# A two-layer decoder trunk: the next stage's first weight slot ahead of the third norm, x turned in four banks, conditioning steps respread, matrix heads scaled on ScalarE

## What is computed

```
mod = silu(c) @ ada_w[layer] + ada_b[layer]        # six rows of 1024: shift, scale, gate twice
h   = x * (1 + scale) + shift
y   = mixer(h)   or   (silu(h @ w1) * (h @ w3)) @ w2
x   = LayerNorm(alpha * x + (1 + gate) * y) * g + b
```

```
num, den = weighted sums over the past            # den from a column of ones
hid = num / max(|den|, exp(-m))
out = sigmoid(o) * head_norm(hid) * ml_g           # mean and variance over the 128 of a head
y   = concat(gla_out, out) @ w_out
```

## Time and profile before

| | |
|---|---|
| median of 3 runs (lowest, highest) | 1455.12 us (1454.17, 1455.47) |
| the profiled execution | 1455.61 us |
| its span | 1453.8 us |
| mean granted TensorE clock | 0.968 |
| TensorE matmul busy | 1369.1 us (94%) |
| VectorE busy | 635.6 us (44%) |
| GpSimd busy | 512.0 us (35%) |
| ScalarE busy | 453.2 us (31%) |

### The profile page before, as it was taken

One profiled execution on the slowest core, in us unless ns is written; L12 is line 12 of the kernel. 1 busy time (PEld: TensorE's weight loads), 2 busy tenths in 40 slices (PEclk: granted clock), 3 DMA queues, 4 the chain that ended last, 5 costly groups with the idle time before them and its releaser, 6 DMA issues.

```text
span 1453.8 us, 17178 instructions
## 1 busy us (share of the span) xinstructions
PE 1369.1 (94%) x6566; PEld 1130.1 (78%) x6566; DVE 635.6 (44%) x835; ACT 453.2 (31%) x606; POOL 512.0 (35%) x209
## 2 busy tenths in 40 slices
PE   7899999979999999999899999998889999999995
PEld 6778777759888888888788777788678888887884
DVE  3579635779443343400882243357484011010007
ACT  2343243424222223122422344315243232232121
POOL 2343312223434435444244222120225444444440
PEclk9999999999999999999999999998999999999998
DMA  9592524241654646743225311111113232334312
GB/s 332 147 121 83 202 101 79 97 166 52 231 194 152 231 167 208 176 128 102 106 102 192 120 48 40 58 44 44 58 58 104 100 101 90 98 97 139 96 58 58
DMA packets 93521, 173.81 MB, mean 120 GB/s; under 512 B 15719, under 2 KB 61943, under 8 KB 93340
## 3 DMA queue, kind: packets, MB, share of 16 engines
q1 hardware_dynamic: 90328, 169.63, 37.7%
q10 hardware_dynamic: 3140, 3.43, 0.8%
HBM read 170.87 MB, written 4.52 MB: 121 GB/s over the span
## 4 chain that ended last, share of the span: by engine, by line
PE 67%; issue 21%; POOL 6%; DVE 5%; ACT 1%; POOLq 0%; DVEq 0%; ACTq 0%
PE ps L1043 13%; PE ps L1044 13%; PE ps L1045 13%; PE ps L1075 6%; PE ps L1076 6%; PE ps L1077 6%; POOL w_lo L677 6%; PE ps L1199 1%; PE ps L1532 1%; PE ps L1200 1%; PE ps L1201 1%; PE ps L1558 1%; PE ps L1546 1%; PE ps L1543 1%; DVE rec L2224 1%
## 5 line engine op out<-in xcount | busy, mean ns | idle before, releaser
L677 POOL TENSOR_TENSOR w_lo<-raw,w_hi 128x1024 fp32r<-128x1024 f32 x205 | 511.8, 2500 | 906.6 <-ACT w_hi L697 906.0
L1043 PE MATMUL ps<-h_lo,w_hi 128*128 128x512 f32 (+2 forms) x1064 | 403.3, 379 | 13.8 <-DVE tmp L1997 7.5
L1044 PE MATMUL ps<-h_hi,w_hi 128*128 128x512 f32 (+2 forms) x1064 | 398.9, 375 | 0.0
L1045 PE MATMUL ps<-h_hi,w_lo 128*128 128x512 f32 (+2 forms) x1064 | 398.5, 375 | 0.0
L697 ACT ACTIVATE w_hi<-raw 128x1024 fp32r<-128x1024 f32 x205 | 216.0, 1056 | 479.9 <-PE ps L1077 172.6
L1043 PEld LDWEIGHTS ps<-h_lo,w_hi 128*128 128x128 f32 (+1 forms) x1064 | 204.6, 192 | 54.7 <-DVE tmp L1997 8.8
L1045 PEld LDWEIGHTS ps<-h_hi,w_lo 128*128 128x128 f32 (+1 forms) x1064 | 204.7, 192 | 35.0
L1044 PEld LDWEIGHTS ps<-h_hi,w_hi 128*128 128x128 f32 (+1 forms) x1064 | 205.0, 193 | 34.0
L2081 DVE TENSOR_TENSOR tmp<-tmp,ps 128x512 f32<-128x512 f32 x44 | 30.1, 687 | 263.1 <-PE ps L1045 263.1
L1075 PE MATMUL ps<-w_hi,hid_lo 128*128 128x512 f32 x352 | 138.0, 392 | 1.8 <-issue 0.9
L1076 PE MATMUL ps<-w_hi,hid_hi 128*128 128x512 f32 x352 | 137.6, 391 | 0.0
(11 more groups left out here) (239 smaller groups left out, 1587.3 us busy)
## 6 DMA issues: line engine op xcount, KB each, us to landing
raw<-wstream SPq DMA_DIRECT2D x205, 512.0 KB, 4.0
ada_raw<-astream SPq DMA_DIRECT2D x80, 512.0 KB, 4.4
ada_first<-astream SPq DMA_DIRECT2D x16, 256.0 KB, 6.9
ada_first<-astream SPq DMA_DIRECT2D x8, 512.0 KB, 10.2
ln_rows<-row_scratch SPq DMA_DIRECT2D x3, 1024.0 KB, 6.7
skew_scratch<-f_scratch ACTq DMA_DIRECT2D x1, 2304.0 KB
xa<-xT SPq DMA_DIRECT2D x4, 512.0 KB, 8.6
out<-xa SPq DMA_DIRECT2D x4, 512.0 KB, 3.5
```

The lines of the kernel that those rows point to most:

```text
L677: nc.gpsimd.tensor_tensor(w_lo[:, slot, :], raw[:, slot % RAW, :], w_hi[:, slot, :].bitcast(F32), ALU.subtract).then_inc(sem("w_lo_ready"), 1)
L1043: pe.matmul(o, w_h, x_l, start=start, stop=False)
L1044: pe.matmul(o, w_h, x_h, start=False, stop=False)
L1045: return pe.matmul(o, w_l, x_h, start=False, stop=stop)
```

## The change

- At each of the first three joints ScalarE rounds the next stage's first weight slot before `normalize(2)`, not behind it.
- `x` is turned into four banks (4 to 7) instead of two, none behind the first slot of `vb`, then three, three and two chunks (`X_BESIDE`). `x_chunk` moves behind `conv_silu(3)`. `gla_o` waits for the copy of the bank it writes.
- `ADA_BESIDE` issues step loads 26 to 29 one slot earlier, 32 and 33 three, 34 and 35 two; 30, 31 and 36 to 39 stay behind their slot. Of block 3, one of three steps of heads 0 and 1 moves behind `ml_stats`. Of block 4, steps 32 and 33 go ahead of `cat_tmp(0)`, 34 and 35 between the chunks, and four stay at the end.
- `ml_gate`'s five VectorE operations for each head become one. ScalarE does num * rstd - mean * rstd (`ml_scaled`, 16 activations of 128 x 128), with the offset from one new small VectorE operation.
- `turn_in(4)` to `turn_in(7)` move up by one k-chunk in `out0_opening`.

```diff
+    X_BESIDE = ((), (0, 1, 2), (3, 4, 5), (6, 7))
...
-                  30: (26, 27), 31: range(28, 32), 35: (32, 33), 36: range(34, 40)}
+                  29: (26, 27), 30: (28, 29), 31: (30, 31), 32: (32, 33), 34: (34, 35), 36: range(36, 40)}
...
-            nc.scalar.activation(xa[:, n, :, :].rearrange("q t c -> q (t c)"), ps[:, 6 + n % 2, :], ACT.Copy).then_inc(sem("xa_ready"), 1)
+            nc.scalar.activation(xa[:, n, :, :].rearrange("q t c -> q (t c)"), ps[:, 4 + n % 4, :], ACT.Copy).then_inc(sem("xa_ready"), 1)
...
             hi_until(SLOTS["vb"][0] + i + RING)
-            x_chunk(2 * i)
-            x_chunk(2 * i + 1)
             if i == 0:
                 conv_silu(3)
+            for n in X_BESIDE[i]:
+                x_chunk(n)
...
+        def ml_scaled(h):
+
+            act.wait_ge(sem("ml_scale"), 1)
+            for tb in range(TB):
+                c = slice(4 * h + tb, 4 * h + tb + 1)
+                i = nc.scalar.activation(num[:, h, tb, 0:P], num[:, h, tb, 0:P], ACT.Identity, scale=rstd[:, c], bias=cols[:, 5, c])
+            i.then_inc(sem("ml_scaled"), 1)
...
+        ml_scaled(0)
         hi_until(out0 + 4)
+        for h in range(1, 4):
+            ml_scaled(h)
...
-            for tb in range(3):
-                normalize(tb)
+            normalize(0)
+            normalize(1)
...
             hi_until(n0 + 1)
+            normalize(2)
...
-                    turn_x(2 * i)
-                    turn_x(2 * i + 1)
+                    for n in X_BESIDE[i]:
+                        turn_x(n)
...
-            if n >= 2:
-                pe.wait_ge(sem("xa_ready"), n - 1)
+            if n >= 4:
+                pe.wait_ge(sem("xa_ready"), n - 3)
...
-            if tb == 2:
-                pe.wait_ge(sem("xa_ready"), 7)
+            if tb < 3:
+                pe.wait_ge(sem("xa_ready"), tb + 5)
...
-                if k == 2:
+                if k == 1:
                     turn_in(4)
                     turn_in(5)
-            turn_in(6)
-            turn_in(7)
+                if k == 2:
+                    turn_in(6)
+                    turn_in(7)
...
-            for tb in range(TB):
-                o = og[:, tb, S + h * P:S + (h + 1) * P]
-                i = V.scalar_tensor_tensor(o, num[:, h, tb, 0:P], mv2[:, 4 * h + tb, 0:1], o, ALU.subtract, ALU.mult)
-            link(i)
+            dve.wait_ge(sem("ml_scaled"), h + 1)
             o = og[:, :, S + h * P:S + (h + 1) * P]
-            V.tensor_tensor(o, o, rstd[:, 4 * h:4 * h + 4].unsqueeze(2).to_broadcast([P, TB, P]), ALU.mult
-                            ).then_inc(sem("og_ready"), 1)
+            V.tensor_tensor(o, o, num[:, h, :, 0:P], ALU.mult).then_inc(sem("og_ready"), 1)
...
-                ada_block(3, False, range(2 + 3 * h, 5 + 3 * h))
+                ada_block(3, False, range(2 + 3 * h, 4 + 3 * h))
+                ml_stats(h)
+                ada_block(3, False, range(4 + 3 * h, 5 + 3 * h))
             else:
                 gla_gate((0, 1))
-            ml_stats(h)
+                ml_stats(h)
...
         mod_block(3)
+        ada_block(4, False, range(0, 2))
...
+        V.scalar_tensor_tensor(cols[:, 5, :], mv2[:, :, 0], -1.0, rstd[:], ALU.mult, ALU.mult).then_inc(sem("ml_scale"), 1)
         cat_tmp(2)
         cat_tmp(3)
+        ada_block(4, False, range(2, 3))
+        cat_lo(2)
+        cat_lo(3)
+        ada_block(4, False, range(3, 4))
         ml_gate(0)
         ml_gate(1)
-        cat_lo(2)
-        cat_lo(3)
+        cat_tmp(4)
         ml_gate(2)
-        cat_tmp(4)
+        cat_tmp(5)
         ml_gate(3)
-        cat_tmp(5)
         cat_lo(4)
...
-        ada_block(4, False)
+        ada_block(4, False, range(4, KC))
```

More of the change, by code:

```diff
@@ L1219, in turn_x @@
                 pe.wait_ge(sem("st_ready"), 14)
-            if n >= 2:
-                pe.wait_ge(sem("xa_ready"), n - 1)
+            if n >= 4:
+                pe.wait_ge(sem("xa_ready"), n - 3)
             for tb in range(TB):
-                m = pe.transpose(ps[:, 6 + n % 2, tile_of(tb)], x_in[:, n, tile_of(tb)], ident)
+                m = pe.transpose(ps[:, 4 + n % 4, tile_of(tb)], x_in[:, n, tile_of(tb)], ident)
             m.then_inc(sem("x_turned"), 1)
```

## The result

The changed kernel takes 1438.81 us (median of 4 runs, 1437.54 to 1442.19) against 1454.64 us for the kernel before in the same session. The ratio is 0.9895, 95% interval 0.9878 to 0.9913. A second session with an unaltered copy gave 1440.53 us (5 runs, 1438.87 to 1440.86), ratio 0.9899 (0.9883 to 0.9914). The forecast was 1440 us. The profiled execution took 1437.54 us with a span of 1435.7 us.

The account below looks back on a forecast made before the run. TensorE, busy 94% of the span, was taken to bound the kernel. Terms 4.6 + 4.4 + 1.4 + 1.8 + 3.8 - 0.6 - 0.3 = 15.1 us off 1455.61 gave 1440.5, or 1440 against the median; range 1434.5 to 1447 us.

Parts of the forecast that it names:

- clock term: Low clock behind three TensorE waits (first transpose of x, `ml_a`, `ada_cols`), claimed gone: 1.7 us each, 5.1 us together.
- x turned later: At the first transpose of x, TensorE's 2.95 us wait and 1.7 us of low clock go: 4.6 us gained.
- a sign of being wrong: The prediction is wrong if the clock falls elsewhere instead, or TensorE waits over 1 us for the sigmoids before `out0`.
- rival (b): Waits go but are partly refound: 1445 us without the clock gains, 1448 without two middle terms as well; chance 0.15.
- Steps respread: In `ml_num(1)`, the 2.7 us wait for `weigh(1)` and 1.7 us of low clock go: 4.4 us gained.
- Rival (c): The respread does nothing, the load for `weigh(1)` still being late: 4.4 us less gain, 1444.5 us; chance 0.08.
- Sigmoids ahead of `out0`: Before `out0`, `cat_tmp(0)` and the sigmoids come late, costing 0.5 us; block 2's 1.9 us wait goes: net 1.4 us.
- Four steps fewer: At the end of `out0`, two steps instead of five run among the last four splits: 1.8 us gained.
- The wait at `ada_cols` and its clock: At the end of `out0`, the 2.1 us wait at `ada_cols` and 1.7 us of low clock go: 3.8 us.
- First turn of joint 0: VectorE has no lead there, so TensorE waits as at the other two joints: 0.6 us lost.
- The joints: At three joints a GpSimd split holds `nmr`, so the stall moves: 0.1 us slower each, 0.3 us lost.
- Rival (a): `nmr` isn't held by the split at the three joints: 20.8 us gained in all, 1434.5 us; chance 0.12.

Follow-up runs that it names:

- the part alone: The kernel before with only the conditioning steps and their loads spread as in the changed kernel: 1445.72 us, ratio 0.9944.
- the joint edit undone: The changed kernel with the third normalisation put back ahead of the weight slots at the three joints: 1439.66 us, ratio 0.9897.
- the joint edit alone: The kernel before with only the third normalisation placed behind the first weight slot at each of the three joints: 1453.17 us, ratio 0.9995.

## Why the prediction came out

The time was right at 1440 us, and but for one clock term by the steps it named. Point by point, each from the first gate group's start (143.51 before, 143.08 after), so that 0.43 us is taken off each difference:

- **x turned later: the wait right, the clock term wrong.** Forecast 4.6 us. At `gla_o` it was 4.7 (173.77 - 168.61 - 0.43), at the negated rows 3.1 (193.43 - 189.89 - 0.43). The 1.7 us of "the low clock behind it, as gone" is the step that failed: the clock fell in 180:190 instead, which the prediction had named as a sign of being wrong. This is the part of rival (b) that came true, and only for this one of the three terms.
- **Steps respread: right.** Forecast 4.4 us. The end of `ml_num(1)` came 7.75 us earlier (225.82 - 217.64 - 0.43), 4.6 more than the negated rows. VectorE took step 28 at 205.80 where the forecast said 206. Rival (c) falls by the part alone.
- **Sigmoids ahead of `out0`: nearly right.** Forecast 0.5 us of loss; `out0` started at 252.42 with a wait of 0.58, and 7.0 us earlier than before (259.84), so 0.8 was lost. Block 2's wait of 1.9 us is gone. ScalarE's activations took 1.64 us for four and 4.73 for twelve, 6.4 in all as forecast, in the idle time as forecast.
- **Four steps fewer: a little less.** GpSimd's last four splits took 11.43 us, not under 11, since the two steps that stayed (38 and 39) took 2.57 and 2.34 us beside them. The last of those slots started 10.3 us earlier (295.73 - 284.97 - 0.43) than before, 3.3 more than `out0`'s start; 1.9 of it is block 2's wait, so 1.4 us are the steps', where the forecast was 1.8.
- **The wait at `ada_cols` and its clock: right.** Forecast 3.8 us. The first turn of the joint started 14.24 us earlier (313.85 - 299.18 - 0.43), so 3.9 more than that last slot. Here the clock term held.
- **First turn of joint 0.** Forecast 0.6 us of waiting, measured 1.10. It isn't a loss of its own: in the changed kernel with the joint edit undone the wait is there, and the joint takes 15.98 us. The forecast's 0.6 us were paid by way of the first slot, as the next point says.
- **The joints: `nmr` held, as forecast.** It takes 2.07 us at the first, 2.08 at the second and 2.08 at the third joint, and `h_lo(2)` is held after it. The second and third joint are 0.1 us longer (16.07 and 16.06 for 15.96 each), as forecast. The first is 0.6 longer (16.56 for 15.95), not 0.1: there `mv` was ready at 303.44, but rounding the slot started only at 303.90, when TensorE, late from the wait at the first turn, gave its place free, and the root came behind it. The rule of the Trainium skill that the prediction weighed ("SBUF — State Buffer", "Who interferes with whom") holds for one column as for a thousand: `nmr` with two inputs in SBUF took 2.07 to 2.08 us. The experiment of one tensor operand is its other half, which the section states for instructions outside the 2-port perf modes: with one input in SBUF, `nmr` takes 0.21 us beside the split.

Up to the fourth residual the change had then won 330.00 - 315.94 - 0.43 = 13.6 us, where my terms give 15.4 less 0.1 for the first joint. Nearly all of the shortfall of 1.7 is the 1.5 of the moved clock; what the sigmoids (0.3) and the last slots (0.4) fall short is mostly made up for by `weigh(1)` (0.2), the wait at `ada_cols` (0.1) and the first joint with its turn (0.6 in all, forecast 0.7). The median's 15.8 us is more than these 13.6. The rest came where the programs are alike but for the held `nmr`, and two executions of one program differ there by as much (3.1 us above), with their clock falls at different waits. The second session's copy is 14.6 us under its own median before. So the forecast's nearness to the median is in part luck, by 1 to 2 us.

Rival (a) priced an unheld `nmr` at 5.4 us and 1434.5 us (its 20.8 us off 1455.1 give 1434.3). The mechanism wasn't in this kernel, but its price was right: with one tensor operand it is 5.4 us by the joints and 1434.89 us by the time.

## What to carry to other kernels

When a VectorE instruction moves under a GpSimd split, don't trust in its being small, and count its tensors in SBUF: here a reciprocal of one column passed, a two-tensor product of one column waited out the split, and the same product written with a scalar column passed. For a large instruction one tensor was no safeguard (2.33 us for 0.75 above). An edit of order can be worth nothing until a second one frees what it runs into; try the pair before dropping either. A stretch of low clock behind a stall is no sure gain from removing that stall: look for other places further on where TensorE waits or does narrow work, and ask more than one execution where the clock falls.

## What the runs showed of the hardware that was not expected

- The granted clock fell to the 1.2 GHz level with no idle time before it: behind, or in the last part of, sixteen one-column matmuls that take 1.95 us at full clock, with 2.3 us of narrow matmuls in front. It did so in the changed kernel and in each experiment that left the sixteen in one run, unless it had fallen at the stall around 152 us. With the sixteen in three groups between full-width matmuls it stayed at 1.00 in the one trace of each of the two kernels that were tried. Behind six other runs of sixteen, with full-width matmuls in front, it stayed at 1.00 too.
- Identical instruction streams (the kernel before and the joint edit alone, up to 190 us) took the fall at different places, at 152 in one and at 188 in the other, each for some 1.7 us.
- A VectorE instruction on one column took 2.08 us beside a GpSimd split when two of its operands were tensors in SBUF, and 0.21 us when one was. One of 128 x 1024 with one such operand took 2.33 us beside a split, and 0.75 us alone.
